# Output products of the delta rule's group 1 moved from group 2 into the last group of a two-layer fp32 encoder trunk

## The reference, cut to what matters

```python
def gated_deltanet(h, w_in, conv_w, a_log, dt_bias, norm_g, w_o):
    proj = h @ w_in
    qkv, z, b, a = jnp.split(proj, [...], axis=-1)
    qkv = jax.nn.silu(causal_depthwise_conv(qkv, conv_w))
    q, k, v = jnp.split(qkv, [B_QK_DIM, 2 * B_QK_DIM], axis=-1)
    ...
    o = chunk_gated_delta_rule(q, k, v, beta, g)      # 16 value heads of 128, 8 query/key heads
    o = o * lax.rsqrt(jnp.mean(o * o, axis=-1, keepdims=True) + RMS_EPS) * norm_g
    o = o * jax.nn.silu(z.reshape(bsz, seq, B_V_HEADS, B_HEAD_DIM))
    return o.reshape(bsz, seq, B_V_DIM) @ w_o         # 2048 x 1024
```

## Time and profile before

| | us |
|---|---|
| median of 3 runs | 1781.0 (1780.4 to 1783.26) |
| the profiled execution, its own time | 1783.87 |
| its span in the profile | 1782.1 |
| TensorE busy in the span | 1698.0 (95%) |
| VectorE / ScalarE / GpSimd busy | 1317.6 / 1062.3 / 177.7 |
| group 0 of the delta rule, from its first transposes (L1628) to those of group 1 | 94.19 |
| group 2, likewise | 99.84 |
| group 3, from its first transposes to the last output products | 88.22 |
| the last output products | 11.26 |

### The profile page before, as it was taken

How to read it: one execution, slowest core, us unless ns; L and a number is a source line. 1 busy time by engine, 2 the same in 40 slices (tenths; PEclk the granted TensorE clock), 3 DMA queues, 4 the chain that set the end, 5 groups by cost and what they waited for, 6 DMA issues and landing times.

```text
span 1782.1 us, 23204 instructions
## 1 busy us (share of the span) xinstructions
PE 1698.0 (95%) x9007; PEld 1438.7 (81%) x9007; DVE 1317.6 (74%) x1065; ACT 1062.3 (60%) x1012; POOL 177.7 (10%) x118
## 2 busy tenths in 40 slices
PE   8799999989999988899999999999999999999996
PEld 7679998878888877778888888888888888888884
DVE  5644445494756656279889889899898898898986
ACT  4443434554546353266777777777777777777773
POOL 0100000044442616100000000000000000000000
PEclk9699999999999999999999999999999999999998
DMA  9136555342221200359999999999999999999992
GB/s 353 38 131 205 184 177 183 97 140 72 72 95 48 71 1 1 148 195 351 351 365 351 348 368 361 352 360 364 359 353 349 374 350 351 368 360 346 369 363 106
DMA packets 155423, 437.91 MB, mean 246 GB/s; under 512 B 9281, under 2 KB 40417, under 8 KB 155361
## 3 DMA queue, kind: packets, MB, share of 16 engines
q1 hardware_dynamic: 155360, 437.03, 68.0%
HBM read 435.95 MB, written 1.05 MB: 245 GB/s over the span
## 4 chain that ended last, share of the span: by engine, by line
PE 84%; DVE 10%; ACT 3%; issue 2%; DMA 0%; POOL 0%; SPq 0%; DVEq 0%; ACTq 0%; POOLq 0%
PE bank L1328 24%; PE bank L1330 24%; PE bank L1329 24%; DVE wlo L844 2%; PE bank L1696 2%; PE bank L1707 2%; PE bank L1809 1%; ACT whi L521 1%; PE bank L1714 1%; DVE TT L1119 1%; DVE T L1097 1%; DVE cvall L1036 1%; PE bank L1832 0%; DVE wlo L1164 0%; PE bank L1833 0%
## 5 line engine op out<-in xcount | busy, mean ns | idle before, releaser
L1164 DVE TENSOR_TENSOR wlo<-raw,whi 128x2048 fp32r<-128x2048 f32 x336 | 767.5, 2291 | 111.0 <-ACT whi L745 107.7
L745 ACT CAST whi<-raw 128x2048 fp32r<-128x2048 f32 x336 | 643.4, 1916 | 244.3 <-PE bank L1330 244.1
L1328 PE MATMUL bank<-whi,xhi 128*128 128x512 f32 (+1 forms) x1584 | 576.6, 364 | 10.8 <-DVE wlo L844 3.5
L1330 PE MATMUL bank<-whi,xlo 128*128 128x512 f32 (+1 forms) x1584 | 568.6, 359 | 0.0
L1329 PE MATMUL bank<-wlo,xhi 128*128 128x512 f32 (+1 forms) x1584 | 568.1, 359 | 0.0
L1328 PEld LDWEIGHTS bank<-whi,xhi 128*128 128x128 f32 x1584 | 301.2, 190 | 57.1 <-DVE wlo L844 4.3
L1330 PEld LDWEIGHTS bank<-whi,xlo 128*128 128x128 f32 x1584 | 300.9, 190 | 44.0
L1329 PEld LDWEIGHTS bank<-wlo,xhi 128*128 128x128 f32 x1584 | 301.4, 190 | 41.4
L844 DVE TENSOR_TENSOR wlo<-raw,whi 128x2048 fp32r<-128x2048 f32 x75 | 186.6, 2491 | 109.0 <-ACT whi L521 108.6
L1328 PE MATMUL bank<-whi,ehhi 128*128 128x512 f32 x448 | 178.5, 398 | 1.8 <-DVE ehlo L1179 1.8
L521 ACT CAST whi<-raw 128x2048 fp32r<-128x2048 f32 x75 | 142.9, 1905 | 58.4 <-PE bank L1330 54.5
(11 more groups left out here) (266 smaller groups left out, 1644.7 us busy)
## 6 DMA issues: line engine op xcount, KB each, us to landing
raw<-in_moe_w_gate_dram SPq DMA_DIRECT2D x112, 1024.0 KB, 6.4
raw<-in_moe_w_up_dram SPq DMA_DIRECT2D x112, 1024.0 KB, 6.5
raw<-in_moe_w_down_dram SPq DMA_DIRECT2D x112, 1024.0 KB, 6.4
raw<-in_dn_w_in_dram SPq DMA_DIRECT2D x24, 1024.0 KB, 5.2
raw<-in_ffn_w_gate_dram SPq DMA_DIRECT2D x11, 1024.0 KB, 5.4
raw<-in_ffn_w_up_dram SPq DMA_DIRECT2D x11, 1024.0 KB, 5.9
raw<-in_ffn_w_down_dram SPq DMA_DIRECT2D x11, 1024.0 KB, 5.0
raw<-in_dn_w_o_dram SPq DMA_DIRECT2D x8, 1024.0 KB, 5.1
```

Source lines behind the costliest of these rows:

```text
L745: act.copy(slot(whi, n, SPLIT), slot(raw, n, RAW)).then_inc(hi_ready, 1)
L1164: dve.tensor_tensor(slot(wlo, n, SPLIT), slot(raw, n, RAW), slot(whi, n, SPLIT).bitcast(F32), ALU.subtract).then_inc(lo_ready, 1)
L1328: pe.matmul(ps, lhs_hi, wh, start=start, stop=False)
L1330: return pe.matmul(ps, lhs_lo, wh, start=False, stop=stop)
```

## The change

The output products of group 1 leave group 2 and stand in group 3, ahead of those of group 2; the second half of group 2's products stands behind the loop, around the last transposes. Group 2 now has group 0's rows of FILLED and AHEAD. Since the gated values of group 1 are read until late in group 3, those of group 2 get a second place, in `xhi` and `xlo`. The four runs of dummy matmuls in this stage are removed. The last output products use banks 2 to 5 in place of 4 to 7.

```diff
--- before.py
+++ after.py
@@ -268,8 +268,10 @@
             for m in range(6):
                 if g + 1 < GROUPS:
                     project_panel(g + 1, m)
-                if g and m in (1, 3):
-                    out_panel(g - 1, m // 2)
+                if g == 1 and m in (1, 3):
+                    out_panel(0, m // 2)
+                if g == GROUPS - 1 and m < 4:
+                    out_panel(1 + m // 2, m % 2)
         for h in range(2):
             out_panel(GROUPS - 1, h)
         P_MOE = len(panels)
@@ -299,9 +301,12 @@
             return again * NE + (NE - 1)
 
         FILLED = ((2, 3, 4, 5, 6, 7, 7, 8, 9, 10, 11, 12, 12, 12), (2, 3, 4, 5, 6, 8, 9, 10, 11, 12, 13, 14, 15, 16),
-                  (2, 3, 4, 5, 6, 8, 9, 10, 11, 12, 13, 14, 15, 16), (0, 0, 1, 2, 3, 4, 4, 4, 4, 4, 4, 4, 4, 4))
-        AHEAD = ((4, 5, 6, 6, 7, 7, 8, 8, 9, 9), (4, 5, 6, 7, 8, 8, 9, 9, 10, 11), (4, 5, 6, 7, 8, 8, 9, 9, 10, 11),
-                 (3, 3, 4, 4, 4, 4, 4, 4, 4, 4))
+                  (2, 3, 4, 5, 6, 7, 7, 8, 9, 10, 11, 12, 12, 12), (2, 2, 3, 4, 5, 6, 6, 6, 6, 6, 6, 6, 6, 6))
+        AHEAD = ((4, 5, 6, 6, 7, 7, 8, 8, 9, 9), (4, 5, 6, 7, 8, 8, 9, 9, 10, 11), (4, 5, 6, 6, 7, 7, 8, 8, 9, 9),
+                 (4, 4, 5, 5, 6, 6, 6, 6, 6, 6))
+
+        def gated(g):
+            return (xhi[:, 0:4 * SEQ], xlo[:, 0:4 * SEQ]) if g == GROUPS - 2 else (onhi[:, :], onlo[:, :])
 
         def conv_src(t):
             return bank[(4, 5, 2, 3)[t // 2]][:, t % 2 * SEQ:(t % 2 + 1) * SEQ]
@@ -650,7 +655,7 @@
             def outputs_hi(g):
                 for f in range(2):
                     act.wait_ge(sem("on_psum"), 2 * g + f + 1)
-                    act.copy(onhi[:, f * 512:(f + 1) * 512], bank[f]).then_inc(sem("onhi_ready"), 1)
+                    act.copy(gated(g)[0][:, f * 512:(f + 1) * 512], bank[f]).then_inc(sem("onhi_ready"), 1)
 
             for part in range(2):
                 hi_panels.upto(P_IN + 2 * part + 3)
@@ -1018,7 +1023,8 @@
                 for f in range(2):
                     dve.wait_ge(sem("onhi_ready"), 2 * g + f + 1)
                     s_ = slice(f * 512, (f + 1) * 512)
-                    dve.tensor_tensor(onlo[:, s_], bank[f], onhi[:, s_].bitcast(F32), ALU.subtract).then_inc(sem("onlo_ready"), 1)
+                    hi_, lo_ = gated(g)
+                    dve.tensor_tensor(lo_[:, s_], bank[f], hi_[:, s_].bitcast(F32), ALU.subtract).then_inc(sem("onlo_ready"), 1)
 
             def add_outputs(g, h, first_bank):
                 dve.wait_ge(panel_used, WO[g, h] + 1)
@@ -1051,6 +1057,8 @@
                 else:
                     lo_panels.upto(LIST[0] + 2)
                 conv_taps(g, 1)
+                if g == GROUPS - 1:
+                    add_outputs(1, 0, lambda b, h: 6 + b).then_inc(sem("outputs_added"), 1)
                 dve.wait_ge(sem("qk_squares"), g + 1)
                 dve.tensor_reduce(ss8, qkT, AX_X, ALU.add).then_inc(sem("qk_sums"), 1)
                 dve.wait_ge(sem("R_psum"), g + 1)
@@ -1073,8 +1081,10 @@
                     i = dve.tensor_tensor(vb[:, 4 * b:4 * b + 4, :], bank[2 + b].rearrange("p (n f) -> p n f", n=4), be, ALU.mult)
                 i.then_inc(sem("vb_ready"), 1)
                 ahead(0)
-                if g:
-                    add_outputs(g - 1, 0, lambda b, h: 6 + b).then_inc(sem("outputs_added"), 1)
+                if g == 1:
+                    add_outputs(0, 0, lambda b, h: 6 + b).then_inc(sem("outputs_added"), 1)
+                if g == GROUPS - 1:
+                    add_outputs(1, 1, lambda b, h: 6 + b).then_inc(sem("outputs_added"), 1)
                 ahead(1)
 
                 dve.wait_ge(sem("EB_ready"), g + 1)
@@ -1118,8 +1128,10 @@
                             dve.wait_ge(sem("TT0_ready"), 2 * g + b + 1)
                         dve.tensor_tensor(t_, t_, bank[4 + b].rearrange("p (n f) -> p n f", n=4), ALU.subtract)\
                             .then_inc(sem("TT_ready"), 1)
-                    if g and lv == 3:
-                        add_outputs(g - 1, 1, lambda b, h: 6 + b).then_inc(sem("outputs_added"), 1)
+                    if g == 1 and lv == 3:
+                        add_outputs(0, 1, lambda b, h: 6 + b).then_inc(sem("outputs_added"), 1)
+                    if g == GROUPS - 1 and lv == 1:
+                        add_outputs(2, 0, lambda b, h: 6 + b).then_inc(sem("outputs_added"), 1)
                     ahead(2 + lv)
                 for b in range(TB):
                     if b == 0:
@@ -1139,8 +1151,10 @@
                         ahead(9)
             outputs_lo(GROUPS - 1)
             lo_panels.upto(P_MOE - 1)
+            add_outputs(GROUPS - 2, 1, lambda b, h: 6 + b).then_inc(sem("outputs_added"), 1)
+            dve.wait_ge(sem("outputs_added"), 2 * (GROUPS - 1))
             for h in range(2):
-                add_outputs(GROUPS - 1, h, lambda b, h: 4 + 2 * b + h).then_inc(sem("x_ready"), 1)
+                add_outputs(GROUPS - 1, h, lambda b, h: 2 + 2 * b + h).then_inc(sem("x_ready"), 1)
             dve.wait_ge(sem("x_ready"), 6)
             for b in range(TB):
                 i = dve.tensor_tensor_reduce(H3[:, b, :], X[:, b, :], X[:, b, :], 1.0, 0.0, ALU.mult, ALU.add, ms[:, b:b + 1])
@@ -1541,7 +1555,7 @@
                 if i == 0 and g:
                     pe.wait_ge(sem("z_scaled"), g)
                 if i in (4, 8):
-                    if g < 2:
+                    if g != 2:
                         pe.wait_ge(sem(("prj_qk_ready", "prj_v_ready")[i // 4 - 1]), g + 1)
                     else:
                         pe.wait_ge(sem("outputs_added"), 2 * (g - 2) + i // 4)
@@ -1567,20 +1581,22 @@
                     use(nn)
                 for k in range(4):
                     s_ = slice(k * SEQ + b * P, k * SEQ + (b + 1) * P)
-                    i_ = triple(o_, onhi[:, s_], onlo[:, s_], nn, slice(k * 512, (k + 1) * 512), k == 0, k == 3)
+                    i_ = triple(o_, gated(g)[0][:, s_], gated(g)[1][:, s_], nn, slice(k * 512, (k + 1) * 512), k == 0, k == 3)
                 if b == 1:
                     i_.then_inc(panel_used, 1)
 
             def output_between(g, i):
                 if i == 0:
                     pe.wait_ge(sem("onlo_ready"), 2 * g + 2)
-                    if g + 2 < GROUPS:
-                        pe.wait_ge(sem("prj_qk_ready"), g + 3)
+                    if g == 0:
+                        pe.wait_ge(sem("prj_qk_ready"), 3)
+                    elif g == 1:
+                        pe.wait_ge(sem("z_scaled"), GROUPS)
                     else:
-                        pe.wait_ge(sem("z_scaled"), g + 2)
+                        pe.wait_ge(sem("outputs_added"), 4)
                 if i == 2:
-                    if g + 2 < GROUPS:
-                        pe.wait_ge(sem("prj_v_ready"), g + 3)
+                    if g == 0:
+                        pe.wait_ge(sem("prj_v_ready"), 3)
                     else:
                         pe.wait_ge(sem("outputs_added"), 2 * g + 1)
                 output(g, i, bank[6 + i % 2])
@@ -1613,7 +1629,9 @@
                         if g == 0:
                             project(1, k)
                         elif g == GROUPS - 1:
-                            output_between(g - 1, k)
+                            output_between(1 + k // 4, k % 4)
+                        elif g == 2:
+                            project(3, k)
                         elif k in (4, 5, 10, 11):
                             output_between(g - 1, k - 4 if k < 6 else k - 8)
                         else:
@@ -1630,12 +1648,9 @@
                 filling(0)
                 if g == GROUPS - 1:
                     pe.wait_ge(sem("z_scaled"), GROUPS)
-                    keep_clock(5, bank[6])
                 if g:
                     outputs_T(g - 1)
                 filling(1)
-                if g == GROUPS - 1:
-                    keep_clock(14, bank[6])
                 pe.wait_ge(sem("convs_ready"), 2 * g + 1)
                 for t in range(4):
                     for b in range(TB):
@@ -1742,13 +1757,14 @@
                         if b:
                             i = pe.matmul(o_, qdecT[:, m, :], S[:, h, :], start=False, stop=True)
                     i.then_inc(sem("o_psum"), 1)
-            pe.wait_ge(sem("outputs_added"), 2 * (GROUPS - 1))
-            keep_clock(14, bank[6])
+            output_between(GROUPS - 2, 2)
             outputs_T(GROUPS - 1)
-            keep_clock(4, bank[6])
+            output_between(GROUPS - 2, 3)
             pe.wait_ge(sem("onlo_ready"), 2 * GROUPS)
+            pe.wait_ge(sem("S_ready"), GROUPS)
+            pe.wait_ge(sem("v_ready"), TB * GROUPS)
             for i in range(4):
-                output(GROUPS - 1, i, bank[4 + 2 * (i % 2) + i // 2])
+                output(GROUPS - 1, i, bank[2 + 2 * (i % 2) + i // 2])
 
             transposed(X, 3)
             pe.wait_ge(sem("router_ready"), 1)
```

## The result

The changed kernel takes 1795.3 us (median of 4 runs, 1793.0 to 1796.6) against 1782.1 us (4 runs, 1780.4 to 1784.3): a ratio of 1.0072, 95% interval 1.0055 to 1.0089. That is 13.2 us slower; the prediction said 10 us slower. The profiled execution took 1793.02 us, its span is 1791.2, so profile against profile the change costs 9.1 us. The profiled execution happens to be the fastest of the four of the changed kernel, and that of the kernel before (1783.87) stood above its median; the 4 us between 9.1 and 13.2 are in neither profile and are not put down to any stage.

A forecast was written before the change was run, and what follows sets the result against it. TensorE bounds group 2; a chain through VectorE, ScalarE, GpSimd and TensorE bounds group 3. Terms -4.7 + 8.6 + 1.7 + 3.6 + 1.0 = +10.2 us on the 1781.0 median give 1791; range 1785 to 1797.

The forecast's parts named there:

- the clock in the head: Start of group 3: TensorE's pauses bring one stretch at 1.2 GHz, +1.7 us (ends 0 and +5.1).
- the levels: Group 3, level 3: the last panel's late cast and subtraction delay the subtraction from TT, +3.6 us.
- group 2: Four units leave, but group 0's stalls appear; length 95.1 us instead of 99.84, -4.7 us.
- Rival (a): Group 2 saves its whole 11.3 us, with no stall opening: 1784.6 us; chance 0.09.
- Head of group 3: TensorE waits 5 and 4.5 us for VectorE's additions before the third and fifth units; kk starts 8.6 us later.
- Rival (c): Group 3: head pauses and level 3's stall each bring a 1.2 GHz stretch, three more than counted: +15, 1796; chance 0.14.
- End: End of the stage: one unit replaces four dummies, so the last products start later, +1.0 us.
- rival (b): Group 3: additions don't hold TensorE up, level 3 has no late subtraction; faster, -2.1 or -3.8 us (1777); chance 0.07.
- The removal of the dummies: Group 3: the removed dummies stood in waits and cost nothing themselves; only the clock was priced.

The follow-up runs named there:

- the second measurement: The changed kernel run once more with no edit: 1793.5 us against 1782.4 for the kernel before, ratio 1.0068.
- the kernel with both panels late: Changed kernel with early additions, group 3's last-but-one panel at place 8 and last panel split behind its outputs: 1775.3 us; second set 1777.4.
- the run with both repairs: Changed kernel with both additions early and group 3's last panel at place 8, fourth at place 1: 1777.5 us against 1782.7 before, ratio 0.9973.

## Why the prediction was right

The direction and the mechanism were right. Three terms were mis-sized, and that the sum still came out is partly luck: the clock in the head was 3.3 us too small, the levels 3.0 and group 2 1.6 us too high. The terms as measured add up to 9.0 us between the profiles (with 0.4 for kk, L1684, which took 2.33 us in place of 1.89 behind the unit at the low clock), the profiles differ by 9.1, and the medians by 13.2 and, in the second measurement, 11.1 us.

- *Group 2, said -4.7, measured -6.3.* The step was to take group 0's 94.19 us. Its two stalls came as read (2.41 and 1.35). What differed is where the stretch of low clock fell: in the changed kernel's group 0, with the same code as before, it fell at the end of the wait for qdec (0.57 from 388.30 to 391.70), and the group took 92.65 us. The second set of the kernel with both panels late had it on level 1 and its group 2 took 95.11 us (553.10 to 648.21), the forecast's 95.1. So the term has a spread of 1.5 us, and where the clock falls is all that the profiles show to differ. Rival (a), the whole 11.3, did not come.
- *Head of group 3, said +8.6 for the chain, measured +8.4.* The additions ended 17.0 and 33.6 us into the group (said 16.9 and 31.2, the difference being the first unit at half clock). TensorE waited 4.90 and 4.19 us, said 5 and 4.5. The run with the additions early shows that moving these two and nothing else removes it.
- *The clock in the head, said +1.7 for one stretch, measured +5.0.* This is the step that was furthest off in size. I took half of 3.4 us per stretch and one stretch, and so kk came 38.9 us into the group and not 34. Both pauses were followed by low clock over a whole unit, and a unit at half clock costs 2.5 us more. The dummies in the waits gave it back. The Trainium skill (TensorE: Matmul & The Clock Gate, section "What's actually happening") calls the low clock the default, which activity lifts. The trace agrees for these two pauses of over 4 us; of the wait of 2.42 us at level 1 it shows both, low clock behind it in the kernel before and full clock in the changed one.
- *The levels, said +3.6, measured +0.6 (35.95 us from L1711 to L1735 against 35.38).* Level 3 itself grew from 5.06 to 8.28 us, +3.2 as argued, and by the way argued: GpSimd's product ran to 711.5 and VectorE's subtraction ended 2.1 us behind it, at 713.7. But the stretch of low clock that the kernel before had at these levels was gone, and with it 2.6 us of cost (levels 1 and 2: 12.99 us against 15.64). I had left that at today's value, without a reason. The levels have no low clock now and the head has two stretches. Rival (c) wanted a stretch behind the stall at level 3 too; none came there, and it is right for the head only.
- *End, said +1.0, measured +0.9* (14.86 us from the last transposes to the end of the products, against 13.92).
- *Faster, rival (b).* Its condition, units 2 and 4 waiting under 1 us together and no subtraction at level 3, is what the run with both repairs brings about (waits of 0 and 0.38 us), and there the kernel is faster by 5.1 us.

The removal of the dummies was costed at nothing but the clock. Taken alone, it costs 3.2 us in the kernel before; in the changed kernel units stand in three of their four places, so how much of its 11 to 13 us is due to them was not separated.

## What to carry to other kernels

Work that is moved into the waits of a chain brings its consumers with it: here two additions on the engine that the chain needs next, and two panels to prepare. Before moving it, place each of them in the order of its engine and ask which unit waits for it. If the reuse of a buffer makes the next unit wait, give the consumer the first gap after the producer, and move preparation out of the chain's narrowest part (levels with no filling) to where its engine is idle anyway. Check the donor too: the covered stage gives back less than the work removed, since stalls that the work hid come out.

## What the hardware showed that I had not expected

- Where a pause was filled or removed, the low clock behind it went, but some came back at another place. The kernel before had one stretch (6.8 us) in group 3, at the levels. The changed kernel has two, both in the head (0.53 from 658.00 to 669.00, 0.57 from 678.00 to 686.00), and none at the levels; with the additions early or with dummies in the waits two came back at the levels. The amount is not fixed: with both repairs one is left. Of the 5.0 us that the dummies gave at the head 3.8 were left at the end of the last products and 2.7 between the medians.
- From the first matmul of the experts to the end, the same code lasted between 1005.9 and 1009.4 us in twelve profiles. The four that took over 1009 had a granted clock of 0.93 to 0.97 in the first 50 us of it, and seven of the other eight had 1.00; what decides it was not looked into. So a single profile can't show a difference of under 3 us in the total; the sums by stage can.
- Subtractions beside it make GpSimd's pair of qdec products longer: 2.03 us with none (kernel before, group 3, at 675.89), 4.08 with one, 6.13 with two. The Trainium skill (SBUF — State Buffer, section "SBUF: two separate sides") has a VectorE instruction with two SBUF inputs and a GpSimd one shut each other out for a whole instruction. The trace agrees nearly: each subtraction adds 2.05 us, and it takes 2.29 alone.
